# Expert units of 64 rows in two halves of the array, or of 32 rows in four quarters

## What is computed

```
gu = xb @ w_gate_up[e] + b_gate_up[e]            # 1024 -> 2048
x_glu = minimum(gu[:, ::2], 7);  x_lin = clip(gu[:, 1::2], -7, 7)
act = x_glu * sigmoid(1.702 * x_glu) * (x_lin + 1)
out = act @ w_down[e] + b_down[e]                # 1024 -> 1024
```

## Time and profile before

| what | value |
|---|---|
| three runs | 1932.15 us median, 1931.82 to 1936.38 |
| the profiled execution | 1936.22 us, its span 1934.7 us |
| busy over the span | PE 1799.1 us (93%), DVE 1024.7 (53%), ACT 795.5 (41%), POOL 240.8 (12%) |
| DMA | 520.06 MB, 269 GB/s on average |
| mean granted TensorE clock | 0.965 of full speed |
| expert stage | 376 to 1535 us of the span |

### The profile page before, as it was taken

One profiled execution on the slowest core, in us unless ns is written; L12 is line 12 of the kernel. 1 busy time (PEld: TensorE's weight loads), 2 busy tenths in 40 slices (PEclk: granted clock), 3 DMA queues, 4 the chain that ended last, 5 costly groups with the idle time before them and its releaser, 6 DMA issues. The chain is left out here.

```text
span 1934.7 us, 41919 instructions
## 1 busy us (share of the span) xinstructions
PE 1799.1 (93%) x14459; PEld 1113.3 (58%) x14459; DVE 1024.7 (53%) x1632; ACT 795.5 (41%) x1163; POOL 240.8 (12%) x302
## 2 busy tenths in 40 slices
PE   5999889589999999999999799999999759998897
PEld 2999754555555555555555355555555436777853
DVE  3785443654555554554454345545455473884665
ACT  3334532244444444444444344444444443433511
POOL 0000000011111111111111011111111120350000
PEclk8999999689999999999999899999999979999999
DMA  7773572249967998799499998999999662221001
GB/s 278 252 249 120 157 204 111 92 171 369 422 257 300 410 427 313 293 421 394 143 404 427 427 427 352 406 427 372 401 426 427 263 231 76 77 77 46 30 30 44
DMA packets 129677, 520.06 MB, mean 269 GB/s; under 512 B 13587, under 2 KB 52260, under 8 KB 80324
## 3 DMA queue, kind: packets, MB, share of 16 engines
q1 hardware_dynamic: 116722, 483.41, 63.9%
q0 software_dynamic: 12736, 35.17, 4.9%
q10 hardware_dynamic: 146, 0.48, 0.1%
HBM read 494.10 MB, written 24.90 MB: 268 GB/s over the span
## 5 line engine op out<-in xcount | busy, mean ns | idle before, releaser
L1878 DVE COPY ring<-staging 128x2048 f32 (+1 forms) x385 | 474.5, 1232 | 508.6 <-PE banks L1739 313.2
L1739 PE MATMUL banks<-ring,rowsT 128*64 128x256 f32 x6144 | 700.7, 381 | 3.4 <-ACT rowsT L1828 3.4
L1739 PEld LDWEIGHTS banks<-ring,rowsT 128*64 128x64 f32 x6144 | 443.3, 138 | 310.7 <-issue 78.5
L1810 ACT ACTIVATE ring<-staging 128x2048 f32 (+1 forms) x193 | 369.0, 1912 | 339.5 <-PE banks L1739 277.5
L1765 PE MATMUL banks<-ring,hiddenT 128*64 128x512 f32 x1536 | 375.4, 610 | 0.5 <-PEq L1796 0.3
L1765 PEld LDWEIGHTS banks<-ring,hiddenT 128*64 128x64 f32 x1536 | 93.8, 137 | 137.2 <-issue 113.0
L1816 ACT ACTIVATE glu<-banks 128x128 f32<-128x128 f32 x192 | 53.2, 277 | 281.1 <-DVE lin L1884 281.1
L586 PE MATMUL banks<-w_in_hi,hT 128*128 128x256 f32 (+1 forms) x768 | 147.8, 292 | 1.0 <-issue 1.0
L2212 PE MATMUL banks<-h3T,w_in_hi 128*128 128x512 f32 x400 | 130.4, 408 | 1.4 <-DVE h3T L2388 1.4
L586 PEld LDWEIGHTS banks<-w_in_hi,hT 128*128 128x128 f32 x768 | 122.9, 194 | 3.0 <-issue 3.0
L1692 POOL DMA_DIRECT2D expert_rows<-y_rows x94 | 52.5, 559 | 527.3 <-ACT y_rows L1834 526.4
(11 more groups left out here) (408 smaller groups left out, 1790.6 us busy)
## 6 DMA issues: line engine op xcount, KB each, us to landing
staging<-in_w_gate_up SPq DMA_DIRECT2D x250, 1024.0 KB, 12.5
staging<-in_w_down SPq DMA_DIRECT2D x128, 1024.0 KB, 12.5
stage<-in_w_mod SPq DMA_DIRECT2D x24, 1024.0 KB, 5.4
stage<-in_w_in SPq DMA_DIRECT2D x25, 512.0 KB, 4.0
expert_rows<-y_rows POOLq DMA_DIRECT2D x94, 128.0 KB, 5.9
stage<-in_w_in SPq DMA_DIRECT2D x11, 1024.0 KB, 6.1
expert_rows<-catT SPq DMA_DIRECT2D x1, 7936.0 KB
early<-in_w_gate_up SPq DMA_DIRECT2D x6, 1024.0 KB, 11.7
```

The costliest lines, as they stand in the source:

```text
L1739: mm = pe.matmul(k.bank(j % 2)[c * SLOTS:(c + 1) * SLOTS, 0:UP], rowsT[:, kk, half, :], w[:, kk * WIDE + c * UP:kk * WIDE + (c + 1) * UP], ...
L1810: act.activation(ring[:, pos % RING, :], staged(e, c), ACT.Copy).then_inc(act_filled, 1)
L1878: dve.tensor_copy(ring[:, pos % RING, :], staged(e, c)).then_inc(dve_filled, 1)
```

## The change

Units have 32 rows (SLOTS 64 to 32). Each unit's rows are the stationary operand on four column quarters of the array, with 128 (up) or 256 (down) columns each; weights and bias are laid out for it on the host. A unit has two steps instead of four: up with two chunks, turn, bias of the next step (now a high and a low part of all 128 partitions, two matmuls), up with two chunks, down with two chunks of the step before. The order of the chunks and of the copies is new to fit. The slot table has 32 x 16 = 512 codes, in int16, from one-hots in the fast float32 format. The pick column no longer comes by DMA for every unit: the router spreads the plan over all partitions with one matmul (`diag`), one compare makes a table `picks` with a column per unit, and `pick_expert` reads a column. The gather takes quarter rows of 1 KB (128 of them, as before of 2 KB), and y is stored in four DMAs of 32 KB instead of two of 128 KB. The places, the ring and the rule of `free` stay as they are.

The core of the diff:

```diff
-SLOTS = 64
+SLOTS = 32
+PARTS = P // SLOTS
...
-    k.slots = k.sb("slots", [P, CODES], I32, at=scope)
+    k.slots = k.sb("slots", [P, CODES], I16, at=scope)
     k.place = k.sb("place", [P, NT, TOPK], at=scope)
     k.inside = k.sb("inside", [P, NT, TOPK], at=scope)
...
+        at_slot = sb("at_slot", [P, 2, TOPK, P], F32R)
+        at_code = sb("at_code", [P, 2, TOPK, CODES], F32R)
+        diag = junk[:, NE * PLACES:NE * PLACES + P]
         past = sb("past", [P, TOPK, PLACES])
-        units = sb("units", [P, NE, PLACES])
+        units = junk[:, 0:NE * PLACES].rearrange("p (e n) -> p e n", n=PLACES)
...
+                pe.wait_ge(unit_diag_ready, 1)
+                pe.matmul(k.bank(7)[:, 0:P], ones_sq, diag, start=True, stop=True).then_inc(units_ps, 1)
...
-                dve.tensor_scalar(k.slots[:], k.bank(2)[:, 0:CODES], 2.0, token[:, NT:NT + 1], ALU.mult, ALU.add)
+                dve.tensor_scalar(k.slots[:], k.bank(2)[:, 0:CODES], float(PARTS), token[:, NT:NT + 1], ALU.mult,
+                                  ALU.add)
...
+                dve.wait_ge(units_ps, 1)
+
+
+STEPS = 2
 WIDE = 2 * UP
-
-POSITION = (0, 1, 3, 4, 6, 7, 8, 9, 10, 11, 14, 17)
+POSITION = (0, 1, 2, 3, 6, 7, 8, 9, 10, 11, 16, 17)
...
+        picks = sb("picks", [P, P])
         pick = sb("pick", [P, P], F32R)
-        picked = sb("picked", [P, LINE])[:, 0:1]
         slot = sb("slot", [P, LINE], I32)[:, 0:1]
-        rows = sb("rows", [P, D // 2])
-        rowsT = sb("rowsT", [P, KT // 2, 2, SLOTS])
-        lin = sb("lin", [P, 2, P])
...
-                def load_picked(i):
-                    after(pool, pick_ready, i)
-                    pool.dma_start(picked, d["picked"][bass.ds(expert_on(pool, i) * P, P), :]).then_inc(picked_in, 16)
-
                 def store_rows(n):
 
                     pool.wait_ge(y_read, n)
-                    for part in range(2):
-                        pool.dma_start(rows_of(part, n * SLOTS - SLOTS), y[part * SLOTS:(part + 1) * SLOTS, :]
-                                       ).then_inc(y_out, 16)
-                    pool.wait_ge(y_out, 32 * n)
+                    for part in range(PARTS):
+                        pool.dma_start(rows_of(part, n * SLOTS - SLOTS), y[of_part(part), :]).then_inc(y_out, 16)
+                    pool.wait_ge(y_out, 16 * PARTS * n)
                     pool.sem_inc(y_free, 1)
 
                 gather(0)
...
-                load_picked(0)
-                load_picked(1)
                 gather(1)
                 with pool.Fori(1, units) as i:
-                    load_picked(i + 1)
                     gather(i + 1)
                     store_rows(i)
                 pool.wait_ge(rows_in, 16 * units + 16)
-                pool.wait_ge(picked_in, 16 * units + 16)
 
             @block.tensor
...
+                    for b in range(2):
                         mm = pe.transpose(k.bank(6)[:, b * P:(b + 1) * P], rows[:, b * P:(b + 1) * P], ident)
                     mm.then_inc(rows_ps, 1)
...
-                    if j == PAIRS - 1:
+                    for low in range(2):
+                        mm = pe.matmul(k.bank(s)[:, 0:UP], pick[:], bias[:, low, s * UP:(s + 1) * UP],
+                                       start=(low == 0), stop=False, skip_group_check=True)
+                    if s == STEPS - 1:
                         mm.then_inc(pick_used, 1)
...
+                def up(i, s, two):
+                    if s == 0 and two == 0:
                         pe.wait_ge(rowsT_ready, i + 1)
                     for half in range(2):
-                        if half:
-                            pe.wait_ge(act_filled, i * len(BY_ACT) + (j + 1))
+                        pos = 6 * s + 2 * two + half
+                        if pos in BY_ACT:
+                            pe.wait_ge(act_filled, i * len(BY_ACT) + (BY_ACT.index(pos) + 1))
                         else:
-                            pe.wait_ge(dve_filled, i * len(BY_DVE) + (2 * j + 1))
-                        w = ring[:, (3 * j + half) % RING, :]
+                            pe.wait_ge(dve_filled, i * len(BY_DVE) + (BY_DVE.index(pos) + 1))
+                        w = ring[:, pos % RING, :]
                         for kk in range(KT // 2):
-                            for c in range(2):
-                                mm = pe.matmul(k.bank(j % 2)[c * SLOTS:(c + 1) * SLOTS, 0:UP], rowsT[:, kk, half, :],
-                                               w[:, kk * WIDE + c * UP:kk * WIDE + (c + 1) * UP],
+                            for c in range(PARTS):
+                                mm = pe.matmul(k.bank(s)[of_part(c), two * P:(two + 1) * P],
+                                               rowsT[:, kk % 2, 2 * half + kk // 2, :],
+                                               w[:, kk * WIDE + c * P:kk * WIDE + (c + 1) * P],
                                                start=False, stop=(half == 1 and kk == KT // 2 - 1),
                                                skip_group_check=True)
                         mm.then_inc(chunk_done, 1)
 
-                def turn_hidden(g, j):
+                def turn_hidden(g, s):
                     if begun(g):
                         pe.wait_ge(hidden_ready, g + 1)
                         after(pe, hT_ready, g - 1)
-                        pe.transpose(k.bank(2 + j % 2)[:, 0:P], hidden[:, j % 2, :], ident).then_inc(turned_ps, 1)
...
-                    pe.wait_ge(dve_filled, i * len(BY_DVE) + (2 * step + 2))
-                    if j == 0:
+                    if s == 0:
                         after(pe, y_read, i)
-                    w = ring[:, (3 * step + 2) % RING, :]
-                    for m in range(2):
-                        for n in range(2):
-                            mm = pe.matmul(k.bank(4)[n * SLOTS:(n + 1) * SLOTS, :], hT[:, j % 2, m * SLOTS:(m + 1) * SLOTS],
-                                           w[:, m * D + n * WIDE:m * D + (n + 1) * WIDE],
-                                           start=(j == 0 and m == 0), stop=(j == PAIRS - 1 and m == 1))
-                    mm.then_inc(chunk_done, 1)
+                    for pos in (first, first + 1):
+                        if pos in BY_ACT:
+                            pe.wait_ge(act_filled, i * len(BY_ACT) + (BY_ACT.index(pos) + 1))
+                        else:
+                            pe.wait_ge(dve_filled, i * len(BY_DVE) + (BY_DVE.index(pos) + 1))
+                        w = ring[:, pos % RING, :]
+                        for m in range(2):
+                            c = 2 * (pos - first) + m
+                            for n in range(PARTS):
+                                mm = pe.matmul(k.bank(4)[of_part(n), 0:part_of], hT[:, s, of_part(c)],
+                                               w[:, m * D + n * part_of:m * D + (n + 1) * part_of],
+                                               start=(s == 0 and c == 0), stop=(s == STEPS - 1 and c == PARTS - 1))
+                        mm.then_inc(chunk_done, 1)
 
                 def steps(i):
-                    for j in range(PAIRS):
-                        g = PAIRS * i + j
-                        up(i, j)
-                        turn_hidden(g - 1, (j - 1) % PAIRS)
-                        if j == 2:
+                    for s in range(STEPS):
+                        g = STEPS * i + s
+                        up(i, s, 0)
+                        turn_hidden(g - 1, 1 - s)
+                        if s == 0:
+                            add_bias(i, 1)
+                        else:
                             turn_rows(i + 1)
-                        if j < PAIRS - 1:
-                            add_bias(i, j + 1)
-                        else:
                             add_bias(i + 1, 0)
-                        down(g - 2, i, (j - 2) % PAIRS)
+                        up(i, s, 1)
+                        down(g - 1, i, 1 - s)
 
                 pe.wait_ge(bias_ready, 1)
...
-                        if j < PAIRS - 1:
-                            fill(i, e, 3 * j + 4)
+                    act.activation(y[:], k.bank(4)[:, 0:part_of], ACT.Copy).then_inc(y_read, 1)
+
+                def steps(i, e_before, e, e_next):
+                    for s in range(STEPS):
+                        g = STEPS * i + s
+                        if s == 1:
+                            if begun(i - 1):
+                                read_y(i - 1, i * CHUNKS + 6)
+                            fill(i, e, 10)
+                        elif e_before is None:
+                            act.wait_ge(act_filled, 1)
+                            act.sem_inc(act_filled, 1)
                         else:
+                            fill(i, e_before, 4)
+                        hidden_turned(g - 1, 1 - s, i * CHUNKS + (6 * s - 6))
+                        if s == 1:
+                            act.wait_ge(chunk_done, i * CHUNKS + 10)
+                            rows_turned(i + 1)
                             fill(i + 1, e_next, 1)
...
```

(35 more changed lines are left out.)

197 lines of the change are left out of this document (82 added, 115 removed).

## The result

The changed kernel took 2080.69 us (median of 4 runs, 2075.30 to 2083.12) against 1931.99 us before: a ratio of 1.0764, 95% interval 1.0734 to 1.0794. I had forecast slower, at 2016 us with a range of 1920 to 2085. The direction and the main mechanism, late rows, came as forecast; the time is 65 us above the forecast. The loss is 149 us where I had 80.

What follows compares the result with a forecast made beforehand. TensorE sets the pace, the weights' queue right behind it. From 1936.2 us, 72 for the expert stage with late rows, 5 for the clock and 3 for the router sum to 2016 us, slower, range 1920 to 2085.

Steps and rivals of the forecast that it cites:

- late rows: Expert stage, row turns: gathers behind y stores come late, unit 14.3 us instead of 12.0, stage 72 us longer; chance 0.54.
- an array that does not work four quarters at full rate: Rival, TensorE: chunk 1.09 us, unit 14.6, time 2033 us, or near 2097 with late rows; chance 0.14.
- 80 units without waits: Expert stage on TensorE: a 32-row unit takes 12.0 us (from below 11.6), so 80 take 960 us.
- waits for weights, start: Expert stage: TensorE's waits for the weights' queue beside late rows, and the stage's start, 55 + 12 us.
- half clock: TensorE at granted clock 0.50 after waits: 5 us lost in all, ends 0 and 25.
- The chain: From last down matmul through y copy, stores, landing, slot copy and gather to landed rows: 19.7 us, full queue.
- "rows in time" rival: Row turns never wait, only the weights' queue is left: 1932 us, or 1919 with 11.6 us units; chance 0.30.
- the bounds I gave for the copies: VectorE's copies per unit: 11.3 us of work fits a 12.0 us unit; ends 12.0 and 12.5 us.
- Four quarters: TensorE matmuls on four column quarters at once: an up chunk takes 0.87 us instead of 1.71.
- The weights' rule: Each expert's first unit waits for its weight transfers, 29.5 us per expert: 1114.4 us with 12.0 us units, 154 waiting.
- Router: Router ahead of the expert stage: wider one-hots, unit sums and slot list add 3 us, ends -3 and +6.

Runs made afterwards that it cites:

- two y buffers and thin weights: Changed kernel with y held twice, picked by unit parity, and only 512 of 2048 columns per weight chunk loaded for experts 4 to 31: 1850.1 us.
- thin copies: Changed kernel loading only 512 of 2048 columns per chunk for experts 4 to 31, each ring copy moving only 1024 of 2048: 1778.1 us.
- the kernel with two y buffers: Changed kernel with y held twice, picked by unit parity, and the landing of the previous stores awaited only ahead of the next stores: 1952.3 us.
- run 4: Not a label: words of "a run 4 us above its median", the profiled execution of the kernel before, nothing changed, 1936.2 us.

## Why the prediction was right, and where it was short

The direction was right and so was the cause that I gave most of the chance to. That 2080.7 us lies in the range is partly luck: it is 4 us below the upper end, and that end was set for another rival, an array that does not work four quarters at full rate. The mechanism forecast 80 us of loss, and 149 were measured.

**The ledger.** From the first to the last unit's start the changed kernel has 1269.5 us, with 13.0 for the last unit 1282.5, and I had forecast 1139 + 72 + 5 = 1216. By terms:

| term | forecast | measured |
|---|---|---|
| 80 units without waits | 80 x 12.0 = 960 | 80 x 12.97 = 1038 |
| late rows | 80 x 2.3 = 184 | 155 |
| waits for weights, start | 55 + 12 | in the next line |
| half clock | 5 | 90, with the start |
| behind the last unit's start, beyond one unit | in the lines above | +13.8 |
| start of the stage, by the span | +3 | -10.4 |

90 is what remains of 1282.5. The late units give the same: they take 21.2 us on average, 8.2 above 12.97, of which 5.2 are wait, and 30 x 3.0 = 91. The spans add up as well: the stage starts 10.4 us earlier, from the first to the last unit's start it is 1269.5 us against 1115.8, 153.7 more, and from there to the end 3.5 more: 146.8, the difference of the spans. These 3.5 hide the 13.8 of the table, since the last unit alone should be 10.3 us shorter than one of 64 rows. In the last unit of the changed kernel the queue is full and the clock half of the time low:

```profile
1652.58:1665.50 12.92, 9.95 (x195) 7.16 (x195) 5.36 (x7) 5.87 (x5) 0.00 (x0) 0.74 1.01 429
```

With two y buffers and thin weights 7 of the 13.8 remain, so about half is the weights and the clock behind them; the rest was not followed.

**Late rows: right.** The wait stands where I put it, ahead of the row turns, in 30 pairs of units, that is 60 of 79, where I had four fifths. The chain is 20.1 us on average against my 19.7. Its parts were less right than the sum, and that they cancel is luck. In the unit shown four issues took 5.4 us and not 2.9, since each meets ring copies for longer than the 0.35 us I charged, and the landing with what follows took 5.45 where I had 7.4 from the rows of 128 KB stores. My "rows in time" rival assumed that the landing would be the part to vanish; with an empty queue the rows were still late. The prediction also speaks of three more issues per unit. It is one more, five where there were four (two stores, the pick and the gather), and the chain was summed with the right five.

**The clock: the step that failed.** I wrote "New waits are shorter but many; ends 0 and 25 us, taken 5." The waits of 5.2 us are not short for the clock: every one of the 30 was followed by half clock, at 3.0 us each. A row of before had shown 5 us lost behind one wait of 6.2. I had the count of the waits from my own sum (a wait of 5.8 in every second unit, some 32 of them) and did not multiply. 32 x 3 would have given 96 and a forecast of about 2107; the 3, though, is hindsight, and with the 5 of that row it is 160 and 2171.

**The unit: 12.97 instead of 12.0.** TensorE's part was right (11.92 with thin copies). It is the second largest miss, 78 us over 80 units, and the bounds I gave for the copies, 12.0 to 12.5, were too low: VectorE is busy for 10.6 of the 13.0 us and late all the same. In order of time, in the late unit shown above but before its wait:

```profile
857.11 2.36 DVE L1887 COPY ring<-staging 128x2048 f32 x2 [1.82 <-PE banks L1738]
```

VectorE stood idle for 1.82 us until TensorE was done with a chunk and so gave a ring place back, and its copy then came 0.41 us late for TensorE (858.39 above). I had compared busy sums, and the limit was the time from a place's release to its use, with four places. A ring of more places was not tried; the staging leaves no room for it.

**Four quarters: right.** The two chunks of an up group start 1.77 us ahead of what follows (855.16 to 856.93 above), 0.88 a chunk where it was 1.71 in two halves: nearly the full factor of two. The Trainium skill, "TensorE: Matmul & The Clock Gate", the section on measured speedup, gives 2.38 for three column tiles and 3.07 for four row tiles. From two halves to four quarters hardly anything of that kind is lost here (a factor of 1.94), and the measurement decides.

**The weights' rule: right, but it did not come to bear.** In the changed kernel the late rows leave the queue time to fill the staging places, and hardly a unit waits for weights. With the rows in time it decides: by the rule with 13.0, 1936.2 + (1147.4 - 1126.5) + 5 - 10.4 = 1951.7, and the kernel with two y buffers took 1952.3. That the two agree within 1 us is chance in part, since the 5 for the clock is my taken one and 1936.2 is a run 4 us above its median. So the rows-in-time rival, which I had at 1932, belonged at about 1952: with this ring and this queue the change would not have been faster even with every row in time.

**Router: wrong sign.** I counted VectorE's wider one-hots (+3) and missed that the stage's start waited for the first pick, whose DMA stood in a full queue. By the waits of the kernel before, VectorE stood 9.4 us for it, once. I had noted that the picks' loads go, and priced them by their issue time on POOL alone.

## What to carry to other kernels

A loop on a queue engine that ends with the wait for its own store makes the next gather as late as that landing; put the wait behind what is issued next, and check this before the step it serves is made twice as short. When a sum says that TensorE will wait several us again and again, price the half clock behind each wait from a row of the trace, and multiply by the count. And a busy sum that fits inside the unit does not show that the copies are in time: with few buffers, follow one copy from the release of its place to its use.

## What the chip showed that I had not expected

Useless work ahead of a wait can pay: 1.8 us of matmuls in each of 79 units took 36 us off, because waits of 5.2 us were followed by 3.0 us of loss at half clock and waits of 0.5 to 1.9 us were not. VectorE, which is busy for 10.6 of a unit's 13.0 us, makes POOL's DMA issues 2.4 times as long (1.22 us on average with full copies, 0.51 with copies half as long), and ScalarE's copies do nothing to them. Four quarter matmuls start 7 ns apart, and the next four 109 ns after the first.
